# An accumulating transfer and six split down slabs in the two feed-forward stages that host a convolution

## The reference

```python
def conformer_conv(h, ...):
    u = h @ w_pw1 + b_pw1
    a, g = jnp.split(u, 2, axis=-1)
    v = a * jax.nn.sigmoid(g)
    v = dwconv(v, w_dw, b_dw)            # depthwise, 31 taps
    v = jax.nn.silu(layernorm(v, ln_g, ln_b))
    ...                                  # then @ w_pw2

# feed-forward: up to 2 x 2816, 3-tap conv, silu(a) * b, down to 1024
```

## Time and profile before

| | |
|---|---|
| median of three executions | 1405.3 us |
| the profiled execution, its own time | 1400.71 us |
| its span | 1399.0 us |
| TensorE busy in the span | 1369.8 us (98%) |
| VectorE, ScalarE, GpSimd busy | 981.1, 824.7, 569.5 us |
| granted TensorE clock | 0.998 of full speed |
| moved by the transfers | 272.04 MB, mean 194 GB/s |

### The profile page before, as it was taken

One profiled execution on the slowest core, in us unless ns is written; L12 is line 12 of the kernel. 1 busy time (PEld: TensorE's weight loads), 2 busy tenths in 40 slices (PEclk: granted clock), 3 DMA queues, 4 the chain that ended last, 5 costly groups with the idle time before them and its releaser, 6 DMA issues.

```text
span 1399.0 us, 27113 instructions
## 1 busy us (share of the span) xinstructions
PE 1369.8 (98%) x10606; PEld 1270.9 (91%) x10606; DVE 981.1 (70%) x1298; ACT 824.7 (59%) x1190; POOL 569.5 (41%) x190
## 2 busy tenths in 40 slices
PE   7999999999999999999999999999999999999997
PEld 4788889999999999999999999999999868999996
DVE  3322684847899987769899979866667596666666
ACT  3632565645788846567888665555554486554554
POOL 2452436455322323452222214655553302366552
PEclk9999999999999999999999999999999999999999
DMA  8775775455344335674444446655554613455551
GB/s 322 253 294 211 268 260 193 153 191 196 138 181 180 158 153 196 246 282 156 161 158 177 181 177 247 239 211 212 212 184 177 268 38 140 174 192 180 180 182 58
DMA packets 39573, 272.04 MB, mean 194 GB/s; under 512 B 4612, under 2 KB 5892, under 8 KB 6974
## 3 DMA queue, kind: packets, MB, share of 16 engines
q1 hardware_dynamic: 39486, 270.81, 52.1%
HBM read 269.73 MB, written 1.06 MB: 194 GB/s over the span
## 4 chain that ended last, share of the span: by engine, by line
PE 78%; DVE 10%; DMA 4%; issue 3%; ACT 3%; POOL 1%; DVEq 1%; SPq 0%; ACTq 0%
PE ps L1982 20%; PE ps L1983 20%; PE ps L1984 20%; PE ps L652 6%; DMA raw<-w_dram 4%; PE ps L2128 3%; DVE sra L1459 2%; PE ps L2019 1%; ACT whi L842 1%; POOL wlo L800 1%; DVE wlo L1337 1%; PE ps L2496 1%; DVE sra L1466 1%; PE ps L2482 1%; PE ps L2029 1%
## 5 line engine op out<-in xcount | busy, mean ns | idle before, releaser
L800 POOL TENSOR_TENSOR wlo<-raw,whi 128x1024 fp32r<-128x1024 f32 (+1 forms) x181 | 567.3, 3137 | 809.1 <-ACT whi L842 809.0
L842 ACT ACTIVATE whi<-raw 128x2048 fp32r<-128x2048 f32 x181 | 345.6, 1911 | 395.8 <-PE ps L1984 223.8
L1337 DVE TENSOR_TENSOR wlo<-raw,whi 128x1024 fp32r<-128x1024 f32 (+1 forms) x181 | 282.7, 1563 | 296.1 <-ACT whi L842 294.9
L1982 PE MATMUL ps<-h_hi,whi 128*128 128x256 f32 x1232 | 354.4, 288 | 1.8 <-ACT gates L999 1.0
L1983 PE MATMUL ps<-h_lo,whi 128*128 128x256 f32 x1232 | 348.7, 283 | 0.0
L1984 PE MATMUL ps<-h_hi,wlo 128*128 128x256 f32 x1232 | 348.7, 283 | 0.0
L1982 PE MATMUL ps<-g_hi,whi 128*128 128x256 f32 x1040 | 298.8, 287 | 2.0 <-POOL wlo L800 1.1
L1983 PE MATMUL ps<-g_lo,whi 128*128 128x256 f32 x1040 | 294.4, 283 | 0.0
L1984 PE MATMUL ps<-g_hi,wlo 128*128 128x256 f32 x1040 | 294.4, 283 | 0.0
L1982 PEld LDWEIGHTS ps<-h_hi,whi 128*128 128x128 f32 x1232 | 236.3, 192 | 10.2 <-issue 6.6
L1983 PEld LDWEIGHTS ps<-h_lo,whi 128*128 128x128 f32 x1232 | 236.4, 192 | 0.8
(11 more groups left out here) (317 smaller groups left out, 1905.6 us busy)
## 6 DMA issues: line engine op xcount, KB each, us to landing
raw<-w_dram SPq DMA_DIRECT2D x243, 1024.0 KB, 4.8
sra<-w_dram SPq DMA_DIRECT2D x2, 1024.0 KB, 6.5
mqk<-w_dram SPq DMA_DIRECT2D x2, 1024.0 KB, 6.4
brev<-w_dram SPq DMA_DIRECT2D x2, 1024.0 KB, 7.2
gates<-w_dram SPq DMA_DIRECT2D x2, 1024.0 KB, 8.5
xlat<-xT_dram SPq DMA_DIRECT2D x2, 512.0 KB, 4.5
brev<-w_first_keys_dram SPq DMA_DIRECT2D x1, 1024.0 KB, 9.2
brev<-bias_rows SPq DMA_DIRECT2D x1, 1024.0 KB, 9.5
```

The costliest lines, as they stand in the source:

```text
L800: pool.tensor_tensor(wlo[:, g.slot, part], raw[:, g.slot, part], whi[:, g.slot, part].bitcast(F32), ALU.subtract).then_inc(lo2_done, 1)
L842: act.activation(whi[:, g.slot, :], raw[:, g.slot, :], ACT.Copy).then_inc(hi_done, 1)
L1337: dve.tensor_tensor(wlo[:, g.slot, part], raw[:, g.slot, part], whi[:, g.slot, part].bitcast(F32), ALU.subtract)\
L1982: pe.matmul(out, w[0], x[0], start=start, stop=False, skip_group_check=True)
```

## The change

Four edits, all for the two hosting stages.

1. Tap products. `PRODUCTS` falls from 22 to 15. Seven taps (`CARRIED`) are made by ScalarE into a buffer of their own, `carried` (the memory of `mqk`), in slot 2 of iteration 1 and slot 1 of iterations 2 to 7, and GpSimd issues a transfer that adds that buffer to a second one, `carried_sum` (the memory of `state`), which it cleared before. VectorE adds the sum once, in iteration 8. VectorE has thus 16 additions a stage where it had 22.
2. Three of the eleven down slabs of each hosting stage, j = 2, 4 and 6, are split. ScalarE gets their `hi` and `m_hi`, VectorE nearly all of their `lo` (1984 words; GpSimd 64) and `m_lo`.
3. GpSimd takes 768 words of the hosting stages' up slabs where it took 512, VectorE 1280 where it took 1536.
4. ScalarE's iterations 2 to 9 are written out one by one, without its loop. SP's and GpSimd's loops over slabs are written out as far as the pattern of whole and split slabs is uneven.

```diff
-PRODUCTS = 22
+PRODUCTS = 15
+ADDED = PRODUCTS + 1
+HOSTS = ("ffn0", "ffn_ctx")
+DOWN_SPLIT = (2, 4, 6)
+CARRIED = 7
...
-            out.append(use != ffn or (i >= 4 and i % 3 == 1))
+            out.append(use != ffn or (i >= 4 and i % 3 == 1 and (i - 4) // 3 not in DOWN_SPLIT))
...
-    if (use, i) == ("wo", 1):
+    if (use, i) == ("wo", 1) or use in DOWN_WHOLE and i >= 4 and i % 3 == 1:
         return 64
+    if use in DOWN_WHOLE:
+        return 768
...
+        carried, carried_sum = flat(mqk[:, :, :, :]), flat(state[:, :, :, :])
...   (ScalarE, split of an iteration)
+                if whole:
+                    act.wait_ge(slab_done, down_slab(b0, j - 2) + 1)
+                    act.activation(m_hi[:, par, :, :], cvb[:, par, :, :], ACT.Copy).then_inc(hostmid_hi, 2)
+                    return
...   (ScalarE, the hosting loop)
-                with act.Fori(0, 3) as jj:
-                    for u in range(2):
-                        up(Slab(b0 + 5 + 3 * u, 2, jj), 2 * jj + (2 + u), u, False)
-                for j in (NJ - 3, NJ - 2):
-                    up(Slab(b0 + 3 * j - 1), j, j % 2, False)
+                for j in range(2, NJ - 1):
+                    g = Slab(b0 + 3 * j - 1)
+                    up(g, j, j % 2, False)
+                    hi(g + (2 + RING))
+                    split(j, j % 2, False)
...   (VectorE, end of an iteration)
+                if whole and host_split(j, par):
+                    dve.wait_ge(hostmid_hi, host_mid(f, j))
+                    dve.tensor_tensor(m_lo[:, par, :, :], cvb[:, par, :, :], m_hi[:, par, :, :].bitcast(F32), ALU.subtract)\
+                       .then_inc(hostmid_lo, 2)
...   (TensorE, down)
+                plain = whole and not host_split(j, par)
+                if plain:
...
+                    if whole:
+                        pe.wait_ge(hostmid_lo, host_mid(f, j))
...   (GpSimd)
+                if use in DOWN_WHOLE:
+                    q = HOSTS.index(use)
+                    run(c, use, 0, 5)
+                    pool.wait_ge(slab_done, done(("pw1_ctx_b", "pw1_lat")[q], (5, 7)[q]))
+                    pool.memset(carried_sum, 0.0).then_inc(carry_zeroed, 1)
+                    k = 5
+                    for j in range(1, 1 + CARRIED):
+                        run(c, use, k, 3 * j + 4)
+                        k = 3 * j + 4
+                        pool.wait_ge(carry_zeroed, q + 1)
+                        pool.wait_ge(carry_made, CARRIED * q + j)
+                        pool.dma_start(carried_sum, carried, accum_op=ALU.add).then_inc(carry_added, 16)
...   (ScalarE)
+            def carried_product(q, j, k):
+                if j > 1 or q:
+                    act.wait_ge(carry_added, 16 * (CARRIED * q + j - 1))
+                made(k, carried).then_inc(carry_made, 1)
...   (ScalarE, slots of conv_act, j <= 7)
+                        if early and at < 2:
+                            product(q, 2 * j + at, 3 * j + (1 + at), (bufA, bufB)[at])
+                        elif early:
+                            carried_product(q, j, CONV_TAPS - 2)
+                        elif at == 1:
+                            carried_product(q, j, 4 * j)
+                        else:
+                            product(q, 2 * j + at // 2, 4 * j + (at - 1), (bufA, bufB)[at // 2])
...   (VectorE, slots of conv_dve)
-                        n = 3 * j + (at - 3)
-                        add_product(q, n, bufs[(par + at + 1) % 2])
-                        if at == 1:
-                            own_tap(q, n + 1, 4 * j + 2)
+                        if at == 0:
+                            add_product(q, 2 * j - 1, bufB)
+                        elif at == 1:
+                            add_product(q, 2 * j, bufA)
+                            own_tap(q, 2 * j + 1, 4 * j + 2)
                     elif (j, at) == (NJ - 3, 0):
-                        add_product(q, PRODUCTS - 1, bufs[(PRODUCTS - 1) % 2])
+                        add_carried(q)
+            def add_carried(q):
+                dve.wait_ge(prod_used, PRODUCTS + ADDED * q)
+                dve.wait_ge(carry_added, 16 * CARRIED * (q + 1))
+                dve.tensor_tensor(flat(acc[:, :, :]), flat(acc[:, :, :]), carried_sum, ALU.add).then_inc(prod_used, 1)
```

More of the change, by code:

```diff
@@ L415, in build @@
         tap0, conv_out, silu_done, mid_f, mid_hi, mid_lo = sem("tap0_done"), sem("conv_done"), sem("silu_done"), sem("mid_done"), sem("mid_hi_done"), sem("mid_lo_done")
+        hostmid_hi, hostmid_lo = sem("host_mid_hi_done"), sem("host_mid_lo_done")
+        carry_zeroed, carry_made, carry_added = sem("carried_sum_zeroed"), sem("carried_product_made"), sem("carried_product_added")
         cond_f, cond_zero = sem("cond_done"), sem("cond_cleared")
@@ L466, in ffn_v, with host_split, host_mid @@
             return (0, 1, 1, 2)[f]
+        carried, carried_sum = flat(mqk[:, :, :, :]), flat(state[:, :, :, :])
+        def host_split(j, par):
+            return j in DOWN_SPLIT if isinstance(j, int) else par == 0
+        def host_mid(f, j):
+            return j + f * DOWN_SPLIT[-1]
         block = ctx.enter_context(nc.Block())
@@ L498, in up @@
                     act.wait_ge(mid_lo, j + (fs * NJ - 1))
+                if whole and isinstance(j, int) and j - 2 in DOWN_SPLIT:
+                    act.wait_ge(hostmid_lo, host_mid(f, j - 2))
                 tap(1, j, par)
@@ L507, in split @@
             def split(j, par, first):
-                if whole:
+                if whole and not host_split(j, par):
                     return
                 act.wait_ge(mid_f, j + (f * NJ + 1))
+                if whole:
+                    act.wait_ge(slab_done, down_slab(b0, j - 2) + 1)
+                    act.activation(m_hi[:, par, :, :], cvb[:, par, :, :], ACT.Copy).then_inc(hostmid_hi, 2)
+                    return
                 if not first:
@@ L637, in down @@
                     pe.wait_ge(lo2_done, g.split() + 1)
-                    pe.wait_ge(mid_lo, j + (fs * NJ + 1))
+                    if whole:
+                        pe.wait_ge(hostmid_lo, host_mid(f, j))
+                    else:
+                        pe.wait_ge(mid_lo, j + (fs * NJ + 1))
                     w = [a[:, g.slot, :].rearrange("p (k n) -> p k n", k=2) for a in (whi, wlo)]
@@ L826, in _ @@
             for use, _, _, count in RUN_ORDER[1:]:
-                run(c, use, 0, count)
+                k = 0
+                if use in DOWN_WHOLE:
[10 more added lines that the diff above has]
+                        pool.dma_start(carried_sum, carried, accum_op=ALU.add).then_inc(carry_added, 16)
+                run(c, use, k, count)
                 c += count
@@ L931, in ln_silu, with made @@
                     upper(KT - 2)
-            def product(q, n, k, buf):
-                if not isinstance(n, int) or n >= 2:
-                    act.wait_ge(prod_used, n + (PRODUCTS * q - 1))
+            def made(k, buf):
                 for t in range(KT):
@@ L939, in product @@
                     ins = act.activation(buf[:, t * T:t * T + T], vpad[:, t, bass.ds(k, T)], ACT.Copy, scale=w)
-                ins.then_inc(prod_done, 1)
+                return ins
+            def product(q, n, k, buf):
+                if not isinstance(n, int) or n >= 2:
+                    act.wait_ge(prod_used, n + (ADDED * q - 1))
+                made(k, buf).then_inc(prod_done, 1)
+            def carried_product(q, j, k):
+                if j > 1 or q:
+                    act.wait_ge(carry_added, 16 * (CARRIED * q + j - 1))
+                made(k, carried).then_inc(carry_made, 1)
             def conv_act(q, out):
                 def host(j, par, at):
-                    if not isinstance(j, int) or j < 2:
-                        early = isinstance(j, int)
-                        if at == 2 and early:
+                    if j < 1 + CARRIED:
+                        early = j < 2
+                        if at == 2 and j == 0:
                             return
@@ L951, in host @@
                             act.wait_ge(pads_done, 2)
-                        n, k = (2 * j + at, 3 * j + (1 + at)) if early else (3 * j + (at - 2), 4 * j + (at - 1))
-                        product(q, n, k, (bufA, bufB)[at if early else (par + at) % 2])
+                        if j == 7 and at == 2:
+                            return
+                        if early and at < 2:
[4 more added lines that the diff above has]
+                            carried_product(q, j, 4 * j)
+                        else:
+                            product(q, 2 * j + at // 2, 4 * j + (at - 1), (bufA, bufB)[at // 2])
                     if isinstance(j, int) and (j, at) == (NJ - 2, 1):
@@ L1130, in tail @@
                 def tail():
-                    act.wait_ge(prod_used, PRODUCTS * (q + 1))
+                    act.wait_ge(prod_used, ADDED * (q + 1))
                     squares(x, bufB, preload=True, ready=(x_ready, ready, 1))
@@ L1502, in ln_sum @@
```

(2 more changed lines are left out.)

4 lines of the change are left out of this document (2 added, 2 removed).

## The result

The changed kernel is slower: median 1414.07 us (1399.64 to 1423.05, 16 executions) against 1401.94 us (1399.06 to 1406.85, 16), ratio 1.0077, 95% interval [1.0059, 1.0094], about 10.8 us. I had forecast 5.9 us less. The longest execution, 1423.05 us, counts as slow and is left out of the ratio; without it the changed kernel's executions scatter over 19 us, those of the kernel before over 8. The profiled execution is one of the shorter ones (1405.37 us, span 1403.5), so it shows the kinds of loss, not their usual size.

A forecast was written before the change was run, and what follows sets the result against it. TensorE's own work was taken as the bound. Six split down slabs save 6.9 us, less 1 us charged for missed deadlines: 5.9 us off 1405.3 gives 1399.4 us, range 1395.5 to 1408.

The forecast's parts named there:

- The gain of a split slab: Hosting stages' down slabs on TensorE: 5.76 us split against 6.91 whole, 1.15 us saved each, 6.9 us for six.
- ScalarE's sum: Hosting stages: an odd and an even ScalarE iteration together take 33.6 us, within TensorE's 35.7 us for the pair.
- VectorE's sum: Hosting stages: VectorE's work per pair of iterations comes to 33.8 us, below TensorE's 35.7 us.
- GpSimd behind VectorE: Hosting up slabs: GpSimd queues behind VectorE's `lo`; its 768 words take 3.4 us in place of 2.85.
- the split slab is late: Rival, chance 0.07: `m_lo` or `lo` queues behind GpSimd, the split slab misses by 1.4 us, no change, 1405 us.
- The transfer: Accumulating transfer in the hosting stages: 5 us of all DMA engines, 7 us to landing; 1 us charged for six pairs.
- E: The end of a whole down slab on TensorE, from which the landings of loads and the deadlines are counted.
- The chain of transfers: Rival, chance 0.14: ScalarE waits to refill `carried`; slower if a transfer exceeds 14.1 us, 1411 us at 15.

The follow-up runs named there:

- e1: The changed kernel without its 14 accumulating transfers, so seven taps of each convolution are missing from the result; ratio 1.0016 to the kernel before.
- e4: The changed kernel with GpSimd's clearing of the sum moved behind slabs 5 and 6 of the stage; ratio 1.0098 to the kernel before.
- e5: The changed kernel without the eight taps of each convolution that VectorE multiplies alone, transfers and split slabs kept; ratio 0.9952 to the kernel before.
- e2: The changed kernel with all down slabs whole again, transfers, 15 products and 768 words kept; ratio 1.0022 to the kernel before.
- e7: The changed kernel with GpSimd back at 512 words of the hosting up slabs; ratio 1.0025 to the kernel before.

## Why the prediction was wrong

- **The gain of a split slab: right.** 5.76 against 6.91 us, and 178.3 us a stage where nothing waits. My 1399.4 us stood on a median of three executions, 1405.3; sixteen give 1401.94.
- **ScalarE's sum: right in size.** Its durations came out as priced, and it was never the engine that TensorE waited for at a down slab.
- **VectorE's sum: the step that failed.** "Per pair: [...] 33.8 us, again below 35.7" took every `lo` at its length when VectorE is first, 1.49 us for 1280 words, and the own taps at 3.26. The working under "GpSimd behind VectorE" asked only how long GpSimd waits, and took from the earlier trace rows that it queues behind. It holds only while VectorE stands ready when ScalarE's `hi` ends, as it did in the earlier trace rows, where it had waited 0.3 to 0.5 us each time. With the split slab's 3 us in front it comes second, and then each `lo` is 3.15 us and the own taps 4.85. As e1's trace has it, a pair is then 33.8 + 2 x 1.66 + 1.59 = 38.7 us, over TensorE's 35.7; the odd iteration is not touched, and TensorE, for which VectorE works ahead, took 36.8 (387.91 to 424.71). It feeds itself within the iteration: VectorE came 0.3 us behind GpSimd at the first `lo` and 1.5 at the second. 768 words made each such wait longer, and I had booked that edit at 0. The rows were there to be seen. One is the mean of 2492 ns for an instruction of 690. Others are in the second hosting stage of the kernel before, which I did not look at: there one `lo` of 1536 words in each of seven iterations running already took 2.82 to 2.85 us in place of 1.76, with GpSimd's part begun before it, and cost TensorE nothing.

```profile
654.30 3.33 POOL L800 TENSOR_TENSOR wlo<-raw,whi 128x512 fp32r<-128x512 f32 x1 [4.25 <-ACT whi L842]
656.42 2.83 DVE L1337 TENSOR_TENSOR wlo<-raw,whi 128x1536 fp32r<-128x1536 f32 x1
```

- **The rival "the split slab is late" had the right mechanism** in the wrong place, at `m_lo`, and a chance of 0.07. I dismissed it because GpSimd has 64 words there, and `m_lo` indeed took 0.81 us, not 2.49; but I did not ask the same of the up slabs. A split slab was late once all the same, for want of its load. The even iteration's transfer goes out some 2.8 us behind the start of a burst (391.06 against 388.25) and meets its second and third load. After the wait at 742.50 TensorE ended its down slab late, the burst began at 751.39, and the transfer, issued at 748.99, was ahead of it. The split slab's own load, the first of the burst, then took 8.05 us in place of 4.8, ScalarE stood idle for it, and TensorE waited 1.5 us for `m_lo`. In e4's trace the same order cost 3.5 us. So one wait of TensorE can bring on the next through the loads.

```profile
759.47 1.91 ACT L887 ACTIVATE whi<-raw 128x2048 fp32r<-128x2048 f32 x1 [7.32 <-DMA raw<-w_dram]
```

- **The transfer: engine time right, consequence half right.** I followed the first up slab of the burst (its second load) and had it land at E + 11. In the changed kernel, with E = 388.25, ScalarE's `hi` of that slab began at 397.08, E + 8.8. The one that came late was the second up slab, the third load, which I had not priced:

```profile
404.43 1.91 ACT L887 ACTIVATE whi<-raw 128x2048 fp32r<-128x2048 f32 x1 [1.33 <-DMA raw<-w_dram]
```

  That is E + 16.2, 1.3 us after ScalarE could have used it. Without the transfers, in e1, the same load landed at E + 9.8. Alone (e5, e2) it costs nothing; on a full VectorE it costs 8.6 us. The Trainium skill's rule that transfers from any engine share the same 16 DMA engines ("DMA: Bandwidth & Descriptors", Issuing engines are not separate DMA queues) agrees with the trace: beside the transfer, which took 14.88 us, this load took 15.26 us, against 8.87 in e1, and the DMA share was 0.90 from 388 to 404 us. The Trainium skill's figure of about half a copy's speed for an adding transfer, stated there for collectives ("Collectives: The Full Stack", The bandwidth ceiling), an estimate of 4.4 us here, is near the 5.1 us of engine time; it says nothing of the 10.9 us to landing.
- **The chain of transfers** did not occur: 14.9 us at the longest, 1.3 us of ScalarE's time in all.
- **Missed: the clock.** I priced a wait at its length. In the second stage two of them, of 2.31 and 2.06 us, were followed by a down slab of 8.8 us in place of 6.91. That can make the cost of waits steeper than their sum. It may, with the two feedbacks above, be why the changed kernel scatters more than twice as far as the kernel before; that is argued, and no run takes the scatter apart.

## What to carry to other kernels

An engine's busy sum against the bound's period is no proof that work fits: two engines that hold each other up have different costs depending on who comes first, and the price in the trace is that of the order it shows. Before loading the engine that is now always early, reprice it as the late one. Where a helper engine has slack, make it wait for the critical one to finish its part; here that single wait was worth 1.1%.

## What the runs showed of the hardware

- VectorE and GpSimd, both subtracting from two SBUF tensors, behaved as if they ran one after the other, whoever came first: VectorE's 1280 words took 1.49 us first and 3.15 second; GpSimd's 768 took 1.86 beside VectorE's taps on PSUM and 3.1 to 3.2 behind VectorE's `lo`, its wait included.
- An accumulating transfer of 1 MB between two SBUF buffers took 5.1 us of the 16 DMA engines, 0.88 us of GpSimd to issue and 8.0 to 14.9 us to land, against 4.9 us in the median for a load of the same size.
- The granted clock fell to 0.72 over 6 us behind waits of TensorE of 2.31 and 2.06 us, and a slab that takes 6.91 us took 8.86. Behind waits of 2.32 us (e4) and 2.02 us (e7) it stayed at 1.00, and the slab took 7.16 and 7.14. What decides between the two is not shown.
